# Two decoder blocks on one core: where the state-space rounds split the z weight, and when cross attention squares k

## The reference, cut to what matters

```python
# first block, cross attention: 4 heads of width 256, 256 memory rows
qn = _rmsnorm(q, gq); kn = _rmsnorm(mk, gk)          # mean square over the head's 256 columns
logits = einsum('bhsd,bhmd->bhsm', qn, kn) * dh ** -0.5
y = einsum('bhsm,bhmd->bhsd', softmax(logits), mv)
# second block, state-space mixer (Mamba-2 form): 8 groups of 4 heads of width 64, state 128
xbc = silu(causal_conv(xbc) + conv_b);  xs, B, C = split(xbc)
decay = exp(where(tril, a_cs[l] - a_cs[s], -inf))     # l, s: positions
y = einsum('bclgn,bcsgn->bcgls', C, B) * decay @ (xs * dt) + d_skip * xs   # one group
y = rmsnorm_per_group(y * silu(z)) * norm_w
```

## Time and profile before

| what | value |
|---|---|
| median of 3 runs | 1271.18 us (1270.01 to 1271.7) |
| the profiled execution's own time | 1270.2 us |
| its span in the trace | 1268.4 us |
| TensorE matmuls busy | 1223.2 us, 96% |
| VectorE busy | 809.2 us, 64% |
| ScalarE busy | 659.8 us, 52% |
| DMA, mean over the span | 166 GB/s |
| granted TensorE clock, mean | 0.989 of full |

### The profile page before, as it was taken

One profiled execution on the slowest core, in us unless ns is written; L12 is line 12 of the kernel. 1 busy time (PEld: TensorE's weight loads), 2 busy tenths in 40 slices (PEclk: granted clock), 3 DMA queues, 4 the chain that ended last, 5 costly groups with the idle time before them and its releaser, 6 DMA issues.

```text
span 1268.4 us, 22328 instructions
## 1 busy us (share of the span) xinstructions
PE 1223.2 (96%) x9844; PEld 1197.3 (94%) x9844; DVE 809.2 (64%) x890; ACT 659.8 (52%) x764; POOL 10.4 (1%) x23
## 2 busy tenths in 40 slices
PE   7999999999999999999989999999989997999996
PEld 6999999999999999999989999999889997999996
DVE  6665666777655557774446577878874555776443
ACT  6443445677543445553334468878764444545330
POOL 0000000000000000000000000000000000000000
PEclk9999999999999999999999999999999998999998
DMA  8553454555656555556555546555446552556540
GB/s 292 168 162 105 134 163 141 146 152 165 200 172 195 166 166 166 176 190 217 182 167 164 178 118 195 167 153 160 156 156 194 194 172 67 181 185 216 183 134 34
DMA packets 210241, 210.28 MB, mean 166 GB/s; under 512 B 6476, under 2 KB 207564, under 8 KB 210144
## 3 DMA queue, kind: packets, MB, share of 16 engines
q1 hardware_dynamic: 207600, 200.30, 50.0%
q0 software_dynamic: 1968, 7.64, 2.1%
q10 hardware_dynamic: 576, 0.90, 0.2%
HBM read 207.73 MB, written 1.09 MB: 165 GB/s over the span
## 4 chain that ended last, share of the span: by engine, by line
PE 75%; DVE 15%; ACT 7%; issue 1%; DMA 0%; DVEq 0%; ACTq 0%
PE ps L236 68%; DVE w_lo L204 6%; PE ps L1390 5%; DVE arena L1020 4%; ACT w_hi L198 2%; DVE arena L1278 1%; ACT L404 1%; ACT arena L766 1%; PE ps L1393 1%; PE ps L245 1%; DVE res L1162 0%; DVE arena L1156 0%; ACT arena L409 0%; DVE arena L1304 0%; DVE arena L1293 0%
## 5 line engine op out<-in xcount | busy, mean ns | idle before, releaser
L236 PE MATMUL ps<-x_hi,w_hi 128*128 128x256 f32 x2752 | 791.6, 288 | 19.2 <-DVE x_lo L1128 9.0
L236 PE MATMUL ps<-x_lo,w_hi 128*128 128x256 f32 x2752 | 781.3, 284 | 0.0
L236 PE MATMUL ps<-x_hi,w_lo 128*128 128x256 f32 x2752 | 781.2, 284 | 0.0
L204 DVE TENSOR_TENSOR w_lo<-raw,w_hi 128x2048 fp32r<-128x2048 f32 x188 | 430.1, 2291 | 231.1 <-ACT w_hi L198 231.1
L236 PEld LDWEIGHTS ps<-x_hi,w_hi 128*128 128x128 f32 x2752 | 530.4, 193 | 26.8 <-issue 21.8
L236 PEld LDWEIGHTS ps<-x_lo,w_hi 128*128 128x128 f32 x2752 | 530.7, 193 | 0.8
L236 PEld LDWEIGHTS ps<-x_hi,w_lo 128*128 128x128 f32 x2752 | 530.6, 193 | 0.0
L198 ACT CAST w_hi<-raw 128x2048 fp32r<-128x2048 f32 x188 | 355.9, 1899 | 117.6 <-PE ps L236 115.6
L236 PE MATMUL ps<-w_hi,x_hi 128*128 128x256 f32 x240 | 69.1, 288 | 2.5 <-DVE w_lo L204 2.5
L1390 PE MATMUL ps<-arena 128*128 128x256 f32 (+3 forms) x448 | 68.1, 341 | 3.1 <-ACT arena L747 2.6
L236 PE MATMUL ps<-w_lo,x_hi 128*128 128x256 f32 x240 | 67.9, 283 | 0.0
(11 more groups left out here) (176 smaller groups left out, 696.5 us busy)
## 6 DMA issues: line engine op xcount, KB each, us to landing
raw<-in_w_in SPq DMA_DIRECT2D x170, 512.0 KB, 4.7
raw<-in_w_ff SPq DMA_DIRECT2D x64, 512.0 KB, 4.5
raw<-in_w_up SPq DMA_DIRECT2D x32, 512.0 KB, 4.7
raw<-in_w_down SPq DMA_DIRECT2D x32, 512.0 KB, 4.4
raw<-in_w_mem_kv SPq DMA_DIRECT2D x16, 512.0 KB, 4.6
raw<-in_w_out SPq DMA_DIRECT2D x16, 512.0 KB, 4.7
raw<-in_w_ssm_proj SPq DMA_DIRECT2D x16, 512.0 KB, 4.6
raw<-in_w_x_proj SPq DMA_DIRECT2D x8, 512.0 KB, 4.5
```

Source lines behind the costliest of these rows:

```text
L204: nc.vector.tensor_tensor(w_lo[:, s], raw[:, s], w_hi[:, s].bitcast(FP32), ALU.subtract)\
L236: last = nc.tensor.matmul(dst, l, r, start=start and k == 0 and m == 0, stop=stop and k == nk - 1 and m == 2)
```

## The change

Five edits. In the state-space rounds ScalarE makes z's high half right after the conv's silu, before the square, z's silu, the table load and decay, where it stood after decay. VectorE makes z's low half between inputs and mask, where it stood after the mask. In cross attention the square of k and the addition of its pair become instructions of their own, placed in the round before (after the softmax's exp on ScalarE, after q's evacuation on VectorE); the q pair is squared and added at the head of the round as before. The semaphores `c_sq` and `c_pair` count two per head. No product, no DMA and no byte changes.

```diff
+            def cross_square_k(i):
+                evacuated(act, cross_units(i)[0])
+                A(c_sq[:, 0:2], c_kq[:, 0:2], ACT.Square).then_inc(S("c_sq"), 1)
             cross_v(0)
+            cross_square_k(0)
@@ ScalarE, cross(i, j)
-                k, q, _ = cross_units(j)
-                evacuated(act, k)
-                evacuated(act, q)
-                A(c_sq, c_kq, ACT.Square).then_inc(S("c_sq"), 1)
+                evacuated(act, cross_units(j)[1])
+                A(c_sq[:, 2:4], c_kq[:, 2:4], ACT.Square).then_inc(S("c_sq"), 1)
...
                 last.then_inc(S("c_p"), 1)
+                if i < 4:
+                    cross_square_k(i)
                 split()
@@ ScalarE, state-space, before the rounds
             ssm_silu(0)
+            split()
             ssm_z(0)
             ssm_exponents(0)
             tables()
             ssm_decay(0)
-            split()
@@ VectorE, cross attention
+            def cross_pair(j, n):
+                dve.wait_ge(S("c_sq"), 2 * j + n + 1)
+                tt(c_sq[:, 2 * n], c_sq[:, 2 * n], c_sq[:, 2 * n + 1], ALU.add).then_inc(S("c_pair"), 1)
+            cross_pair(0, 0)
             def cross(i, j):
-                dve.wait_ge(S("c_sq"), j + 1)
-                tt(c_sq[:, 0:4:2], c_sq[:, 0:4:2], c_sq[:, 1:4:2], ALU.add).then_inc(S("c_pair"), 1)
+                cross_pair(j, 1)
...
                 evac(U("cross", i, 1, 3), c_kq[:, 2:4])
+                if i < 4:
+                    cross_pair(i, 0)
                 split()
@@ TensorE
-                pe.wait_ge(S("c_pair"), j + 1)
+                pe.wait_ge(S("c_pair"), 2 * j + 2)
```

## The result

The changed kernel takes 1257.24 us (median of 4 runs, 1256.4 to 1259.04), the kernel before 1270.6 us in the same series: a ratio of 0.9896, 95% interval 0.988 to 0.9912, 13.4 us faster. Two later series gave 0.9893 (0.9879 to 0.9906) and 0.9899 (0.9885 to 0.9912). The prediction said 1259.3 us, 11.9 us faster, and its range was 1255.8 to 1264.5. (A series is a set of runs taken together.)

A forecast was written before the change was run, and what follows sets the result against it. The prediction took a loop of VectorE and ScalarE to bound the state-space rounds. Rounds, first group and exit together -10.6 us, cross attention -1.3, in sum -11.9: 1259.3 us, range 1255.8 to 1264.5.

The forecast's parts named there:

- The bound and the rounds: State-space: VectorE-ScalarE loop sets 22.65 us; without z's low half 20.39, so TensorE binds at 20.99; five rounds give -8.3 us.
- The first group loses: First state-space group: ScalarE had no wait to fill, so decay, mask and values come later: +1.1 us, between 0 and 1.9.
- The exit: After the last round: the 3.57 us stop and 1.7 us of half clock go, a new 2.2 us stop appears.
- Cross attention: Three of four heads lose their 0.22 us pair stop and 0.25 us of refill, the first gains nothing: -1.3 us.
- The clock: Stops of 2.4 us before the first group's values and 2.2 us at the exit: no half clock, nothing counted.
- B: State-space rounds: a second loop, ScalarE's list with the added split, binds at 21.5 us a round: 1261.9 us; chance 0.15.
- C: First group's values and exit: half clock follows both longer or new stops: 1262.7 us; chance 0.09.
- D: State-space rounds: TensorE waits for mask or silu instead of the weight, so rounds give nothing: 1268 us; chance 0.08.
- E: State-space rounds: ScalarE's moved split waits for a late raw z load, holding everything behind it: slower, 1279.7 us; chance 0.05.

The follow-up runs named there:

- the halves alone: Two runs of the changed kernel: with only ScalarE's half of z's split moved, 1269.81 us; with only VectorE's half moved, 1283.45 us.
- the added squares: The changed kernel with the square of y on ScalarE done four times instead of once in each group: 1269.11 us.
- the repetition: The changed kernel itself run and profiled once more, with no edit: 1257.03 us.

## Why the prediction was right, point by point

**The bound and the rounds: right, 0.5 us too small.** That a loop without a matmul set 22.65 us and that TensorE would bind next is shown by the halves alone and by the added squares. From the second group's scores to the last ones it is 134.26 us before and 125.40 us after: -8.9 us, forecast -8.3. The difference is 0.09 us in each of six rounds: I took the one round of 20.99 us for TensorE's own pace, and that is 20.90. At its end silu was done at 801.23 and the scores began at 801.28, so probably even that round was held for a moment by the loop.

**The first group loses: right.** From TensorE's arrival at the values to the next scores it is 14.43 us before (765.86 to 780.29) and 15.41 us in the repetition at full clock (763.35 to 778.76): +1.0, forecast +1.1. In the first trace it is 16.90 us, +2.5: the half clock of that execution.

**The exit: right.** The forecast was a return at 921.8 us and a stop of 2.2 us; the first trace has 921.56 and 2.07. From the last scores to the return it is 17.82 us before and 14.24 us after: -3.6, forecast -3.35.

**Cross attention: right.** From the first pair sums to the fourth 67.46 us before and 66.12 after: -1.34, forecast -1.4 for three heads. From the restart near 22 us to the first pair sums it is 15.63 us before and, in the repetition at full clock, 15.70: +0.07, forecast +0.1. The stop there is shorter (0.51 against 0.71 us) without a gain, for TensorE came to it later. That the k square, which now stands ahead of ScalarE's next splits, is the cause would fit (VectorE waited 1.23 us for a high half, 1.02 before), but was not tried by itself.

Added up, -8.9 + 1.0 - 3.6 - 1.3 = -12.8 us at full clock, where the forecast has -11.9.

**The clock: the step that was off.** "I count nothing for the two" new stops. One trace of before had shown full clock behind 2.45 us and half clock behind 3.57 us, and I read that as the length deciding. The same trace had a third row, passed over: half clock behind 2.89 us near 664 us. The Trainium skill ("TensorE: Matmul & The Clock Gate", "HAM oscillation") did not settle it either: it tells of an engine that waits for transfers again and again, each time for longer than the 2.3 and 2.1 us here, and does not say that a single stop as short as these is followed by half clock. The runs show that it can be: behind the first stop in 4 of 7 traces, behind the second in 2 of 6, at 1.5 us each, so some 1.4 us on average (an estimate, 1.5 x (4/7 + 2/6)). That the total was still within 2 us is in part luck, for the forecast was 0.9 us too small in the other terms.

The clock also misleads the comparison of two single traces: it is 11.2 us between the profiled executions and 13.4 between the medians, and the first trace after had half clock at two places where the trace before had none. The trace before against the second one after, which has none of these falls, gives 14.0 us of span. The terms above cover 12.7 of it. The traces differ by 0.2 us at the restart near 22 us, and by 0.95 us between 664 us and the first values, where no edit reaches: half clock behind the 2.89 us stop lasts longer in the one (a granted clock of 0.50 over 5 us) than in the other (0.70). So the agreement of -12.8 us with the medians' -12.9 to -13.4 is not exact bookkeeping; about 1 us of it hangs on where the clock falls, and how much of that is in the medians stays open.

**The rivals.** B, the loop with ScalarE's list in it as the new bound: no, but it was only 0.5 us away, and 2.0 us added to that list made it the bound. C, half clock behind the new stops: in part, above. D, the stop only changes its name: no, the rounds have no stop left. E, a split that cannot start holds up what stands behind it: the load was not late here, but the mechanism is real, and with only VectorE's half moved it cost 13 us.

## What to carry to other kernels

Where rounds are longer than the bounding engine's busy time, find the cycle of waits and take out of it what need not be there; work moved into another engine's wait must have its own input ready there, so the two halves of a pair move together or not at all. After that, price what the same move does in the first and the last round, where there was no wait to fill: restoring the first and moving one more split at the exit gave another 4.5 us in the medians, 3.1 us in traces at full clock. A short stop on TensorE may cost its half clock in one execution and not in the next, so compare medians, or traces whose clock rows agree.

## What the runs showed of the hardware that was not expected

A stop of 2.07 to 2.45 us was followed by half clock in 9 of 26 cases, at a cost of 1.3 to 1.5 us. It was not the place that decided: in three traces of the changed kernel the clock fell at two of the three places, at none, and at the third. Stops of 3.51 to 3.92 us were followed by half clock in 4 of 4 cases, and one of 2.89 us with one of 0.60 us just ahead of it in 13 of 13; but one of 3.35 us was not. The changed kernel's four runs in the first series lie between 1256.4 and 1259.04 us.

A stop of 0.22 to 0.62 us costs about 0.25 us beyond its idle time (22.48 against 22.01 us for a cross head with one stop of 0.22 us; 22.65 against 20.90 us for a round with two of 1.15 us together, 0.3 us each). The rows show where it is. The profile counts idle time from the shown end of the last matmul, 0.28 us after its start, though the next would have started after 0.12 us: 0.16 us that the idle time leaves out. And behind the stop of 0.24 us in the kernel before the second matmul starts 0.19 us after the first, not 0.12.

```profile
931.85 0.28 PE L236 MATMUL ps<-x_hi,w_lo 128*128 128x256 f32 x1
932.37 0.35 PE L236 MATMUL ps<-x_hi,w_hi 128*128 128x256 f32 x1 [0.24 <-DVE w_lo L204]
932.56 0.28 PE L236 MATMUL ps<-x_lo,w_hi 128*128 128x256 f32 x1
```
